# Two down projections of an MLP: seven block products in place of eight, on two of eight row groups of the weights

## The chip, the cores and the metric

One core of a Trainium2 chip runs the whole program. The metric is the device time of one execution in microseconds; the number given for a kernel is the median of several runs.

## The reference, cut to what matters

The program is one block with three attention branches, followed by two small transformer layers on 256 tokens of width 1024. Each of the two layers ends with the same MLP, and the change is in its second product:

```python
def sq_relu_mlp(x, w_up, w_down):
    h = jax.nn.relu(x @ w_up)
    return (h * h) @ w_down
```

x is 256 x 1024, w_up 1024 x 4096, w_down 4096 x 1024, all in float32. The result goes through a norm with a gain and is added to x.

## The kernel before

**Float32 by three products.** Every weight and every operand is cut into a rounded high part and a low part, the rest. A product is then high x high, high x low and low x high, three matmuls that add up in one PSUM bank. For a weight, ScalarE writes the high part `Wh` (`split`, L1294 to L1303) and VectorE subtracts it from the raw copy to get the low part `Wl` (`split`, L1828 to L1833).

**Granules and the ring.** The weights come from memory as one stream of granules of 1 MB: four blocks of 128 rows by 512 columns. `raw`, `Wh` and `Wl` have four slots each (`RING` = 4), granule g lies in slot g % 4. SP loads a slot of `raw` when VectorE has split the granule that was in it (`lo_ready`, L500 to L508). ScalarE may write a slot of `Wh` when TensorE has used up the granule four before (`gran_used`). TensorE waits for `lo_ready` of its granule.

**Units.** A unit is 512 output columns for both tiles of 128 tokens, so it owns a pair of PSUM banks `ps` (`bank(name, t)`); units alternate between the two pairs. A granule is 4 blocks x 3 matmuls x 2 token tiles = 24 matmuls of 128x512. `product` (L712) runs a unit granule by granule; `tile_by_tile` (L721) runs the last four granules of a stage first for token tile 0 and then for tile 1, so that the next stage can start on tile 0.

**The MLP.** The up product has eight units of two granules, `up{m}_0` to `up{m}_7` (m is 0 or 1). ScalarE reads each bank into `held` with a relu (L1721) and squares it (L1728). VectorE turns the squared rows in 32x32 blocks into `htmp` (`turn_pair`, L2382, 16 instructions for two units), ScalarE writes the high part `hTh` (`high_pair`, L1730) and VectorE the low part `hTl` (`low_pair`, L2396). The down product has two units of eight granules, `down{m}_0` and `down{m}_1`, 16 in all. Granule q of a unit needs the turned rows of group q (`h_low`). The last rows (groups 6 and 7) are turned and split while `down{m}_0` is already running. When unit 0 is done, ScalarE sums its squares (`down_squares`) and VectorE reads it out with the gain (`gained`); unit 1 ends with `normed_rows` and, in the first MLP, with `cross` into the next stage.

**The order of the work** is written out by hand for each engine and is strictly in order: ScalarE's in `mlp` (L1712), VectorE's in `mlp` (L2379), TensorE's in `mlp` (L1207). In `down{m}_0` both run a loop over the granules and split granule g + 4 while TensorE is at g. GpSimd has almost nothing to do in the MLP: the power -0.5 of the norms and the load of the next gain row (`after_mix`, L633). Four more PSUM banks, `aux0` to `aux3`, are used for transposes and attention, in an order fixed by `plan_aux` (L137); in the MLP they lie idle after the transposes of `x3T` or `x5T`.

## Time and profile before

| | us |
|---|---|
| median of 3 runs | 1108.35 (1107.96 to 1108.49) |
| profiled execution: span from the first to the last instruction | 1106.3 |
| TensorE busy in it | 1098.5 (99%) |
| TensorE weight loads | 913.3 (83%) |
| VectorE busy | 806.6 (73%) |
| ScalarE busy | 636.1 (58%) |
| GpSimd busy | 150.0 (14%) |
| memory read | 203.33 MB, 185 GB/s over the span |

Of the profiled execution only its span is given; the runs' times are from the device and lie 2.05 us above it. Times in the trace are counted from the start of the span. Matmuls overlap, so the mean duration of one (389 ns) is longer than the distance from one to the next; the path is read from the chain. The granted TensorE clock is 1.00 of full speed, 2.4 GHz, throughout. The first MLP's down units run from about 730 to 818, the second's from about 1013 to 1101. The profile marks VectorE as DVE, ScalarE as ACT, GpSimd as POOL, TensorE as PE and its weight load as PEld, and the queue of a sequencer by a q behind it.

### The profile page before, as it was taken

How to read it: one execution, taken by the hardware profiler on the slowest of the kernel's cores; microseconds unless marked ns; L12 is line 12 of the kernel's file. 1: busy time of each engine (PE TensorE's matmuls, PEld its weight loads, DVE VectorE, ACT ScalarE, POOL GpSimd, SP SyncE). 2: the span in 40 equal slices, each digit the busy share in tenths (PEclk: the TensorE clock that was granted, in tenths of full speed). 3: DMA queues.
4: the chain of work that ended last, by engine and by line, in shares of the span. 5: the costliest groups of instructions: out<-in, count | busy, mean ns of one | idle time of the engine just before them, and what ended most of it. 6: DMA issues, size and time to landing. Idle time of an engine off the chain costs nothing.

```text
span 1106.3 us, 13497 instructions
## 1 busy us (share of the span) xinstructions
PE 1098.5 (99%) x5131; PEld 913.3 (83%) x5131; DVE 806.6 (73%) x920; ACT 636.1 (58%) x787; POOL 150.0 (14%) x111
## 2 busy tenths in 40 slices
PE   9999999999999999999999999999999999999997
PEld 7788888888888888888888888888888888888886
DVE  5785768776678873778448569998467976899942
ACT  7656576655767653654587366654355655756431
POOL 1434600000344310000023000000005000000000
PEclk9999999999999999999999999999999999999999
DMA  9645444555455555655435446546555334654530
GB/s 355 247 172 183 144 161 162 200 190 190 186 195 190 190 195 185 229 200 197 183 115 195 166 179 258 188 156 229 193 188 208 122 145 171 225 174 180 191 145 38
DMA packets 30503, 205.16 MB, mean 185 GB/s; under 512 B 3624, under 2 KB 3792, under 8 KB 6768
## 3 DMA queue, kind: packets, MB, share of 16 engines
q1 hardware_dynamic: 28752, 198.75, 49.4%
q0 software_dynamic: 1696, 5.64, 1.6%
q8 instruction: 38, 0.62, 0.2%
q14 instruction: 17, 0.14, 0.0%
HBM read 203.33 MB, written 1.05 MB: 185 GB/s over the span
## 4 chain that ended last, share of the span: by engine, by line
PE 96%; DVE 2%; ACT 1%; issue 0%; DVEq 0%; ACTq 0%
PE ps L685 84%; PE ps L1139 3%; PE aux L757 3%; PE ps L1141 1%; PE ps L800 1%; PE aux L1006 1%; PE aux L1176 1%; PE aux L991 1%; PE ps L877 0%; PE aux L1163 0%; PE ps L793 0%; DVE Wl L1833 0%; ACT Wh L1303 0%; DVE prob L2050 0%; ACT bprob L1777 0%
## 5 line engine op out<-in xcount | busy, mean ns | idle before, releaser
L685 PE MATMUL ps<-Wh,xT 128*128 128x512 f32 x1792 | 560.1, 391 | 0.0
L1833 DVE TENSOR_TENSOR Wl<-raw,Wh 128x2048 fp32r<-128x2048 f32 x183 | 422.6, 2317 | 151.3 <-ACT Wh L1303 150.3
L1303 ACT ACTIVATE Wh<-raw 128x2048 fp32r<-128x2048 f32 x183 | 349.0, 1914 | 187.6 <-PE ps L685 187.5
L685 PEld LDWEIGHTS ps<-Wh,xT 128*128 128x128 f32 x1792 | 336.4, 188 | 69.9 <-issue 0.3
L685 PE MATMUL ps<-Wl,xT 128*128 128x512 f32 x896 | 348.6, 389 | 0.0
L685 PEld LDWEIGHTS ps<-Wl,xT 128*128 128x128 f32 x896 | 168.3, 188 | 34.1
L685 PE MATMUL ps<-Wh,hTh 128*128 128x512 f32 x256 | 99.7, 389 | 0.0
L685 PE MATMUL ps<-Wh,hTl 128*128 128x512 f32 x256 | 99.6, 389 | 0.0
L685 PE MATMUL ps<-Wl,hTh 128*128 128x512 f32 x256 | 99.6, 389 | 0.0
L2392 DVE STREAM_TRANSPOSE htmp<-held 32x512 f32<-32x512 f32 x128 | 90.0, 703 | 2.7
L637 POOL TENSOR_TENSOR sc<-sc,cst 128x1 f32<-128x1 f32 x8 | 4.5, 559 | 443.6 <-DVE sc L2352 443.6
L685 PEld LDWEIGHTS ps<-Wl,hTh 128*128 128x128 f32 x256 | 48.1, 188 | 10.0
L685 PEld LDWEIGHTS ps<-Wh,hTl 128*128 128x128 f32 x256 | 48.0, 188 | 10.0
L685 PEld LDWEIGHTS ps<-Wh,hTh 128*128 128x128 f32 x256 | 48.0, 188 | 9.8
L1139 PE MATMUL ps<-xT,Wh 128*128 128x512 f32 x128 | 45.3, 399 | 0.0
L521 POOL TENSOR_TENSOR sc<-sc,cst 128x8 f32<-128x8 f32 (+1 forms) x11 | 18.0, 1640 | 165.8 <-DVE sc L1900 153.9
L1721 ACT ACTIVATE held<-ps 128x512 f32<-128x512 f32 x32 | 18.8, 594 | 32.8 <-PE ps L685 32.8
L1141 PE MATMUL ps<-xT,Wl 128*128 128x256 f32 x128 | 35.9, 281 | 0.0
L685 PE MATMUL ps<-Wh,ffTh 128*128 128x512 f32 x88 | 34.4, 391 | 0.0
L685 PE MATMUL ps<-Wh,ffTl 128*128 128x512 f32 x88 | 34.3, 389 | 0.0
L685 PE MATMUL ps<-Wl,ffTh 128*128 128x512 f32 x88 | 34.2, 389 | 0.0
L1347 ACT ACTIVATE xT<-aux,gains 128x128 fp32r<-128x128 f32 x80 | 21.8, 384 | 21.6 <-PE aux L757 21.6
(355 smaller groups left out, 1310.6 us busy)
## 6 DMA issues: line engine op xcount, KB each, us to landing
raw<-in_wstream SPq DMA_DIRECT2D x185, 1024.0 KB, 4.8
grow<-in_post_gains POOLq DMA_DIRECT2D x4, 512.0 KB, 6.2
grow<-in_b_gate POOLq DMA_DIRECT2D x6, 256.0 KB, 3.4
mrows<-in_mem SPq DMA_DIRECT2D x2, 512.0 KB, 5.3
raw<-in_wstream SPq DMA_DIRECT2D x2, 512.0 KB, 6.5
x<-in_x SPq DMA_DIRECT2D x1, 1024.0 KB, 13.5
out<-x SPq DMA_DIRECT2D x4, 256.0 KB, 2.0
rdm<-in_ret_decays POOLq DMA_DIRECT2D x1, 768.0 KB, 5.1
```

The lines of the kernel that those rows point to most:

```text
L521: nc.gpsimd.tensor_tensor(S(f"{key}_rstd", 0, n), S(f"{key}_var", 0, n), K("minus_half").broadcast_to([P, n]), ALU.pow).then_inc(sem("norm ...
L685: mm = nc.tensor.matmul(ps[2 * pair + t][:, :], a[:, kt, t * P:(t + 1) * P], w[:, slot, j, :], start=(first and j == 0 and q == 0), stop=( ...
L757: tr = nc.tensor.transpose(o[0:src.shape[1], at:at + P], src, ident)
L800: mm = nc.tensor.matmul(bank("mk", t), a[:, 4 * g + j, t * P:(t + 1) * P], w[:, g, j, :], start=(g == 0 and j == 0 and a is memTh and w is ...
L991: mm = nc.tensor.matmul(o[:, t * TOK + k0:t * TOK + k1], qT[:, h + h0, t * P:(t + 1) * P], kT[:, h + h0, k0:k1], start=True, stop=True)
L1139: nc.tensor.matmul(o[:, :], Wh[:, g % RING, kt % 4, w], xT[:, kt, :, :], start=(kt == 0), stop=False, skip_group_check=True)
L1141: mm = nc.tensor.matmul(o[:, 0:TOK], Wl[:, g % RING, kt % 4, w], xTh[:, kt, :], start=False, stop=(kt == DK - 1), skip_group_check=True)
L1303: nc.scalar.activation(split_view(Wh, g), weight_view(raw, g), ACT.Copy).then_inc(hi_ready, 1)
L1347: nc.scalar.activation(dst[:, k0 + j, t * P:(t + 1) * P], o[:, j * P:(j + 1) * P], ACT.Copy, scale=gcol(gain, k0 + j)).then_inc(sem(f"{nam ...
L1721: nc.scalar.activation(held[:, n // 2, t, n % 2, :], bank(name, t), ACT.Relu).then_inc(drained["act"], 1)
L1833: nc.vector.tensor_tensor(split_view(Wl, g), weight_view(raw, g), split_view(Wh, g).bitcast(F32), ALU.subtract).then_inc(lo_ready, 1)
L2392: i = nc.vector.transpose(dst[b:b + 32, :, :, a:a + 32], src[a:a + 32, :, :, b:b + 32])
```

## The change

In each of the two down products, groups 0 and 1 of the rows of the weights, for both units, are a product of 2x2 blocks: A (two token tiles by two groups) times B (two groups by two units). Before, it is eight block products of 12 matmuls. After, it is seven, Q1 to Q7, by a form of Strassen's scheme, in which the weights are only added:

- the rows: Q1 takes a11, Q2 a12, Q4 a22; Q5 a21-a22, Q6 a11-a21+a22, Q7 a11-a21, Q3 a12-a11+a21-a22. The four mixed ones are made on VectorE (`mix_rows`, four subtractions on 128x512 in the up stage) and cut into high (`mixh`, ScalarE) and low parts (`mixl`, VectorE);
- the weights: Q1 B11, Q5 B11+B12, Q6 B11+B12+B22, Q4 the sum of all four; Q3 B22, Q7 B22+B12; Q2 B21. Q1, Q3 and Q2 are plain loads. Q5, Q6, Q4 and Q7 are transfers that GpSimd issues with an adding write onto the raw slot of the product four positions before (`fast_sums`);
- Q1, Q5, Q6 and Q7 go into the four `aux` banks, ScalarE copies each out (`fast_part`); Q2, Q3 and Q4 are added directly in the units' banks. GpSimd makes four sums of the copies, and VectorE adds them into the four banks (`add_part`): three before the split of the position behind Q7 plus four, one when unit 0 is complete;
- the order of TensorE is (0,2), (0,3), Q1, (1,2), (1,3), (0,4), Q5, (0,5), Q3, Q2, Q6, (0,6), Q7, (0,7), Q4, then granules 4 to 7 of unit 1 tile by tile; (n,q) is granule q of unit n. These are 19 positions of the ring in place of 16. TensorE waits for the added sums of unit 1 before its last four granules;
- SP's loop over the stream becomes a straight list, a plan of positions (`plan_positions`) takes the place of the granule numbers, the head norms share two semaphores, and the loops of VectorE and ScalarE over `down{m}_0` follow the new order.

The diff, cut to its core:

```diff
+FAST_ORDER = [(0, 2), (0, 3), "Q1", (1, 2), (1, 3), (0, 4), "Q5", (0, 5), "Q3", "Q2", "Q6", (0, 6), "Q7", (0, 7), "Q4"]
+FAST_LOAD = {"Q1": (0, 0, False), "Q5": (1, 0, True), "Q6": (1, 1, True), "Q4": (0, 1, True),
+             "Q3": (1, 1, False), "Q7": (1, 0, True), "Q2": (0, 1, False)}
+FAST_BANK = {"Q1": 0, "Q5": 1, "Q6": 2, "Q7": 3}
...
@@ SP
-            with sp.Fori(1, NG // RING) as i:
-                for j in range(RING):
-                    sp.wait_ge(lo_ready, i * RING + (j + 1 - RING))
-                    sp.dma_start(raw[:, j, :, :], by_ring[i, j]).then_inc(landed[j], 16)
...
+            for g in range(RING, NP):
+                if not ADDED[g]:
+                    sp.wait_ge(lo_ready, g + 1 - RING)
+                    sp.dma_start(raw[:, g % RING, :, :], wstream[SRC[g]]).then_inc(landed[g % RING], 16)
@@ GpSimd
+            def fast_sums(m):
+
+                first = P0[f"down{m}_0"]
+                for what in ("Q5", "Q6", "Q7", "Q4"):
+                    g = first + AT[what]
+                    pool.wait_ge(lo_ready, g + 1 - RING)
+                    pool.dma_start(raw[:, g % RING, :, :], wstream[SRC[g]], accum_op=ALU.add).then_inc(added[CHAIN[g]], 16)
+                wait_read(pool, f"fast{m}", FAST_BANK["Q1"])
+                wait_read(pool, f"fast{m}", FAST_BANK["Q6"])
+                nc.gpsimd.tensor_tensor(part6[:, :, :], part6[:, :, :], part1, ALU.subtract).then_inc(sem("fast_sum"), 1)
+                wait_read(pool, f"fast{m}", FAST_BANK["Q5"])
+                pool.wait_ge(sem("fast_sum"), 4 * m + 1)
+                nc.gpsimd.tensor_tensor(partu[:, :, :], part6[:, :, :], part5, ALU.add).then_inc(sem("fast_sum"), 1)
+                wait_read(pool, f"fast{m}", FAST_BANK["Q7"])
+                nc.gpsimd.tensor_tensor(part7[:, :, :], part7[:, :, :], part6[:, :, :], ALU.subtract).then_inc(sem("fast_sum"), 1)
+                pool.wait_ge(sem("fast_sum"), 4 * m + 3)
+                nc.gpsimd.tensor_tensor(part5, part5, part7[:, :, :], ALU.subtract).then_inc(sem("fast_sum"), 1)
@@ TensorE, mlp
-                product(f"down{m}_0", (hTh, hTl), before={q: rows_ready_for(q) for q in range(8)})
-                product(f"down{m}_1", (hTh, hTl), leave=RING)
...
+                fast_product(m, rows_ready_for)
+                before = {(0, 0): lambda: pe.wait_ge(sem("fast_add"), 4 * m + 2)}
@@ TensorE, fast_product, one product Q
+                        for j in range(4):
+                            if what in mixed:
+                                high, low = mixh[:, mixed[what], j, :], mixl[:, mixed[what], j, :]
...
+                            for i, (a, w) in enumerate(((high, Wh), (high, Wl), (low, Wh))):
+                                mm = nc.tensor.matmul(o, a, w[:, g % RING, j, :],
...
@@ ScalarE, mlp
                 for n in range(8):
                     up(n)
+                    if n == 7:
+                        split(P0[n0] + RING)
                     if n >= 3 and n % 2:
                         high_pair((n - 3) // 2)
                     squared_rows(n)
...
+                act.wait_ge(sem("mix_rows"), m + 1)
+                act.wait_ge(gran_used, P0[n0])
+                nc.scalar.activation(mixh[:, :, :, :], mixr[:, :, :, :], ACT.Copy).then_inc(sem("mix_high"), 1)
+                for k in range(1, len(FAST_ORDER)):
+                    if FAST_ORDER[k] in FAST_BANK:
+                        fast_part(FAST_ORDER[k], parts[FAST_ORDER[k]])
+                    elif k == 7:
                         high_pair(3)
...
+                    split(P0[n0] + k + RING)
@@ VectorE, mlp
+                def mix_rows():
+
+                    a11, a12 = htmp[:, 0:4, 0:P], htmp[:, 4:8, 0:P]
+                    a21, a22 = htmp[:, 0:4, P:TOK], htmp[:, 4:8, P:TOK]
+                    link(nc.vector.tensor_tensor(mixr[:, 0, :, :], a21, a22, ALU.subtract))
+                    link(nc.vector.tensor_tensor(mixr[:, 1, :, :], a11, mixr[:, 0, :, :], ALU.subtract))
+                    nc.vector.tensor_tensor(mixr[:, 2, :, :], a11, a21, ALU.subtract)
+                    nc.vector.tensor_tensor(mixr[:, 3, :, :], a12, mixr[:, 1, :, :], ALU.subtract).then_inc(sem("mix_rows"), 1)
...
+                for k in range(1, len(FAST_ORDER)):
+                    if k == AT["Q7"] + 1:
+                        dve.wait_ge(sem("fast_sum"), 4 * m + 4)
+                        add_part(n1, 0, partu[:, :, :])
+                        add_part(n1, 1, part5)
+                        wait_unit(dve, n0, 0)
+                        add_part(n0, 0, part1)
+                    split(P0[n0] + k + RING)
+                    if k in (1, 3, 4):
+                        at0 = {1: 4, 3: 8, 4: 12}[k]
+                        turn_pair(3, at0, at0 + 4)
+                    elif k == 2:
+                        dve.wait_ge(sem("mix_high"), m + 1)
+                        nc.vector.tensor_tensor(mixl[:, :, :, :], mixr[:, :, :, :], mixh[:, :, :, :].bitcast(F32), ALU.subtract)\
+                            .then_inc(sem("mix_low"), 1)
+                    elif k == 6:
                         low_pair(3)
...
+                wait_unit(dve, n0, 1)
+                add_part(n0, 1, part7[:, :, :])
+                gained(p, n0, 0, post_k)()
```

## Rows read from the trace of the kernel before

**Rows 1.** The page's part 4, the chain that ended last, by engine.
```profile
PE 96%; DVE 2%; ACT 1%; issue 0%; DVEq 0%; ACTq 0%
```

**Rows 2.** That chain in order of time, 700 to 925 us: start, duration, what.
```profile
699.96 112.20 PE ps L685 x495
```

**Rows 3.** Waits of PE over the span: total us, times, longest us.
```profile
PE ps L793 <- DVE warm L1934: 1.5, 1, 1.5
PE ps L685 <- DVE byTl L1852: 0.4, 1, 0.4
```

**Rows 4.** Windows: us, busy us (instructions) of PE, PEld, DVE, ACT, POOL, clock, DMA share, GB/s.
```profile
730.00:774.00 44.00, 44.00 (x196) 36.44 (x195) 40.24 (x35) 21.35 (x16) 0.00 (x0) 1.00 0.57 209
774.00:818.00 44.00, 44.00 (x200) 36.53 (x199) 20.25 (x20) 18.31 (x20) 0.56 (x1) 1.00 0.47 167
...
692.00:767.00 75.00, 75.00 (x333) 62.10 (x332) 73.70 (x70) 40.87 (x33) 0.00 (x0) 1.00 0.51 183
```

**Rows 5.** Groups by shape, 730 to 774 us: busy us, mean ns of one, idle before.
```profile
L1833 DVE TENSOR_TENSOR Wl<-raw,Wh 128x2048 fp32r<-128x2048 f32 x9 | 20.5, 2291 | 3.0 <-ACT Wh L1303 2.8
L1303 ACT ACTIVATE Wh<-raw 128x2048 fp32r<-128x2048 f32 x8 | 15.3, 1913 | 12.2 <-PE ps L685 12.2
L2392 DVE STREAM_TRANSPOSE htmp<-held 32x512 f32<-32x512 f32 x21 | 14.8, 703 | 0.4
...
L2401 DVE TENSOR_TENSOR hTl<-htmp,hTh 128x1024 fp32r<-128x1024 f32 x4 | 4.7, 1219 | 0.0
```

**Rows 6.** Groups by shape over the span: a 128x512 bank copy, a 128x512 VectorE product.
```profile
L1721 ACT ACTIVATE held<-ps 128x512 f32<-128x512 f32 x32 | 18.8, 594 | 32.8 <-PE ps L685 32.8
...
L2250 DVE TENSOR_TENSOR rcos<-reo,rtab 128x512 f32<-128x512 f32 x8 | 5.5, 692 | 0.3
```

**Rows 7.** Timeline of DVE in both MLPs: start, us, line, out, in, idle before.
```profile
730.53 2.29 DVE L1833 TENSOR_TENSOR Wl<-raw,Wh 128x2048 fp32r<-128x2048 f32 x1
...
763.35 4.49 DVE L1833 TENSOR_TENSOR Wl<-raw,Wh 128x2048 fp32r<-128x2048 f32 x2
770.68 2.29 DVE L1833 TENSOR_TENSOR Wl<-raw,Wh 128x2048 fp32r<-128x2048 f32 x1 [2.85 <-ACT Wh L1303]
...
1013.57 2.29 DVE L1833 TENSOR_TENSOR Wl<-raw,Wh 128x2048 fp32r<-128x2048 f32 x1
```

**Rows 8.** Timeline of ACT around the start of the first down unit.
```profile
730.60 0.60 ACT L1721 ACTIVATE held<-ps 128x512 f32<-128x512 f32 x1 [2.12 <-PE ps L685]
...
741.53 1.92 ACT L1303 ACTIVATE Wh<-raw 128x2048 fp32r<-128x2048 f32 x1 [1.02 <-PE ps L685]
746.98 1.92 ACT L1303 ACTIVATE Wh<-raw 128x2048 fp32r<-128x2048 f32 x1 [3.52 <-PE ps L685]
```

**Rows 9.** Timeline of DVE in the up stage: the first low_pair and what follows.
```profile
691.72 2.35 DVE L2401 TENSOR_TENSOR hTl<-htmp,hTh 128x1024 fp32r<-128x1024 f32 x2
694.18 2.85 DVE L2392 STREAM_TRANSPOSE htmp<-held 32x512 f32<-32x512 f32 x4
```

**Rows 10.** Timelines of POOL and DVE in the feed-forward stage: 128x512 products beside splits.
```profile
293.54 1.30 POOL L611 TENSOR_TENSOR gu<-gu 128x512 f32<-128x512 f32 x1 [2.83 <-DVE fe L1912]
294.97 3.19 POOL L615 TENSOR_TENSOR fheld<-gu,fe 128x512 f32<-128x512 f32 x1
...
294.34 5.96 DVE L1833 TENSOR_TENSOR Wl<-raw,Wh 128x2048 fp32r<-128x2048 f32 x2 [0.88 <-ACT Wh L1303]
...
336.39 3.28 POOL L611 TENSOR_TENSOR gu<-gu 128x512 f32<-128x512 f32 x1 [7.70 <-DVE fe L1912]
```

**Rows 11.** Transfers to landing: L505 (1 MB, SP); L642, L631 (512 KB, POOL); down window.
```profile
DMA to landing us min/median/max: 4.6/4.8/12.6
...
L642 POOL DMA_DIRECT2D grow<-in_post_gains x3: 572/572/617, 646.2 to 929.9; - x3
DMA to landing us min/median/max: 6.1/6.3/9.8
...
DMA to landing us min/median/max: 4.0/4.0/4.0
...
q1 hardware_dynamic: 1263, 9.17, 56.4%
```

More of the change, by code:

```diff
@@ L431, in build @@
         landed = [sem(f"landed{i}") for i in range(RING)]
+        added = [sem(f"added{i}") for i in range(2)]
         hi_ready = sem("hi_ready")
@@ L677, in _, with half_granule @@
         def _(pe):
-            def half_granule(slot, th, tl, kts, pair, t, first, last, ready=None):
+            def half_granule(slot, th, tl, kts, pair, t, first, last, ready=None, mixed=False):
                 for j, kt in enumerate(kts):
@@ L2206, in ff @@
                 name = f"ffn{n}"
[L2207 removed]
+                split(P0[name] + RING)
                 if first:
@@ L2426, in mlp, with add_part @@
                         turn_pair(k, 8, 12)
-                for g in range(G[f"down{m}_0"], GEND[f"down{m}_0"] - 1):
-                    split(g + RING)
-                    q = g - G[f"down{m}_0"]
-                    if q < 3:
-                        turn_pair(3, 4 * q + 4, 4 * q + 8)
-                    elif q == 3:
+                n0, n1 = f"down{m}_0", f"down{m}_1"
+                def add_part(name, t, part):
+                    v = bank(name, t).rearrange("p (k t) -> p k t", t=P)
+                    nc.vector.tensor_tensor(v, v, part, ALU.add).then_inc(sem("fast_add"), 1)
+                for k in range(1, len(FAST_ORDER)):
[14 more added lines that the diff above has]
+                    elif k == 6:
                         low_pair(3)
-                gained(p, f"down{m}_0", 0, post_k)()
-                split(GEND[f"down{m}_0"] - 1 + RING)
-                for g in range(G[f"down{m}_1"], GEND[f"down{m}_1"] - RING):
-                    split(g + RING)
+                wait_unit(dve, n0, 1)
+                add_part(n0, 1, part7[:, :, :])
+                gained(p, n0, 0, post_k)()
                 rows = normed_rows(p, f"down{m}_1", post_k, after)
                 if gain:
-                    cross(GEND[f"down{m}_1"], f"{after}T", gain, rows)
+                    cross(P1[f"down{m}_1"], f"{after}T", gain, rows)
                 else:
```

296 lines of the change are left out of this document (195 added, 101 removed).

## The prediction

> **What bounds the kernel now.** Three views in this order. The chain that ended last lies almost wholly on TensorE [rows 1]. Followed through the first MLP it is one unbroken run of matmuls, 495 in 112.20 us [rows 2], so a matmul costs 0.2267 us of the path (the 389 ns of the groups overlap), a granule of 24 costs 5.44 us and half a granule 2.72 us. TensorE hardly waits for a semaphore anywhere [rows 3]. A matmul that is left out in a down stage is therefore time gained, as long as its weights and operands come as early as before. The third view asks who would be late next. In the windows of the down stage VectorE is busy 40.24 of 44 us and ScalarE 21.35; from the middle of the up stage into the down stage VectorE is busy 73.70 of 75 us; in the second down unit it is busy 20.25 of 44 [rows 4]. So there are two limits close together: TensorE sets the end, and VectorE, in the very stretch that is changed, has almost nothing left.
>
> **What goes.** Per MLP, four granules (units 0 and 1, groups 0 and 1) of 24 matmuls become seven products of 12: 96 become 84. 12 x 0.2267 = 2.72 us per MLP, 5.44 us in both. With all of it: 1108.35 - 5.44 = 1102.9. (Sums are made on the span, 1106.3 us, which lies 2.05 us under the median of the runs; the difference is carried over unchanged.) The granted clock is 1.00 in all the windows [rows 4], so no gain or loss of clock enters.
>
> **What comes.** Time is counted from the start of the first down unit, 730.6, where ScalarE reads the last up bank [rows 8], and TensorE leaves a granule every 5.44 us (741.53, 746.98 there).
> TensorE, never waiting, would start the 15 positions at 0, 5.4, Q1 10.9, 13.6, 19.1, 24.5, Q5 29.9, 32.7, Q3 38.1, Q2 40.8, Q6 43.6, (0,6) 46.3, Q7 51.7, (0,7) 54.5, Q4 59.9, and the last four granules of unit 1 at 62.6. Each position needs its split (ScalarE 1.91, VectorE 2.29 us [rows 5]), and ScalarE may begin it only when TensorE has left the position four before.
>
> VectorE's queue. In the up stage four subtractions on 128x512 are put in (mix_rows), 4 x 0.69 [rows 6] = 2.8 us, and low_pair(0) loses half of one 1.22 us step, 0.5: +2.3 us in a queue without a gap [rows 4, 9]. The split of position 2 thus starts at 2.0 to 2.3 in place of -0.1 [rows 7]. From there to the split of position 11 the queue holds 10 splits x 2.29 (22.9), five groups of four transposes x 2.86 (14.3, from 703 ns each [rows 5]), two low_pairs x 2.35 (4.7) and the low part of the mixed rows, as large as a split (2.3): 44.2 us, done at 46.2 to 46.5. TensorE wants it at 46.3. All earlier positions have 1.6 us or more. So this place costs 0 to 0.2 us; each further microsecond of VectorE work ahead of it would cost nearly one. Before, the same queue ran out and waited for ScalarE only at 767.8 [rows 7].
>
> The accumulating transfers. Four of the seven weight sums are made by transfers of 1 MB that add onto a used raw slot. GpSimd issues each (0.57 us to issue [rows 11]) when VectorE has split the position four before. No row shows an accumulating transfer. The nearest below is a plain one of 1 MB, 4.8 us to landing (up to 12.6); the nearest above, twice the slowest 512 KB transfer of GpSimd, 2 x 9.8 = 19.6 us [rows 11]. In the down stage 9.17 MB took 56.4% of 44 us, 2.8 us of engine time per transfer of 1.05 MB; reading the old slot as well would add that once: 4.8 + 2.8 = 7.6; two full plain passes would be 9.6. I take 8 to 9, nearer the plain row because the size and pattern are the same. The Trainium skill, "Collectives: The Full Stack", Part 3, says of a reducing transfer that the add is free and "the add needs two source reads"; by that the estimate is 7.6 us and the whole gain, 1102.9; no run here shows it yet.
>
> What landing time L is allowed? Q5 has over 20 us, Q6 and Q7 about 12. The tight one is Q4. It is asked for when position 10 is split, at 41.5, issued by 42.5, and lands at 42.5 + L. ScalarE stands in its queue at this split; behind it stand the split of 15, the copy of Q7's bank (0.6 [rows 6]) and the split of 16: 3 x 1.9 + 0.6 = 6.3. Then VectorE splits 16 (2.3) and only then adds the shared sums into unit 1's two banks (2 x 0.69), for which TensorE waits before position 15. 42.5 + L + 6.3 + 2.3 + 1.4 = 52.5 + L against 62.6: a stall from L = 10.1 on, if GpSimd is quick.
>
> GpSimd's four sums of 128x512 take 1.30 us when VectorE stands or transposes, but 3.19 and 3.28 us beside a split, and two splits beside them took 5.96 in place of 4.49 us [rows 7, 10]. The last two sums (1.3 to 3.3 each) must lie between the copy of Q7, 55.1 at the earliest, and the adds: 57.7 to 61.7, plus 1.4, is 59.1 to 63.1 against 62.6. And each hit lengthens VectorE's queue by up to 1.3 us just where it works through 13 to 16; two of them move the point where the stall starts from L = 10.1 to about 7.5. So at L = 8 the stall is 0 to 0.6 us per MLP, at 9.6 it is 0 to 2.2. I take 0.6 each, 1.2 in all: 1102.9 + 1.2 = 1104.1.
>
> Edits that I cost at nothing, with their cover: the split of position 4 now stands ahead of high_pair(2) on ScalarE and holds it until 7.4, but its rows are wanted at 24.5 instead of 21.8; low_pair(3) ends at about 44 for a position at 46.3 (before it ended 763.3 for one at 763.3). The high part of the mixed rows (1.9 us) lies in ScalarE's idle time. SP's loop becomes a straight list and skips four transfers; its plain loads keep over 4.8 us except position 13 (asked 39.3, wanted 45.0), which may take about 8 us before it costs. On GpSimd the four issues and sums stand ahead of the power step of this MLP, which is wanted only after unit 1. The banks of the four own products are free since the transposes of x3. Unit 1's last granules, and all after them, run as before. The merged semaphores of the head norms change no order. The second MLP has the same queues at the same distances (VectorE's split of position 2 at 1013.57 [rows 7]), so each term counts twice.
>
> **The rivals.**
> 1. Nearly the whole gain: stall under 1.6 us per MLP, 1102.9 to 1106.1, likeliest 1104.1. For it: the counts above; against it: three places with less than 0.6 us of room.
> 2. The saved matmuls are handed back at the adds: L near 10 to 12 or GpSimd's last two sums caught beside splits. Stall 1.6 to 3.8 us per MLP, middle 2.6: 1102.9 + 5.2 = 1108.1, no change. For it: VectorE's full queue and the 3.28 us of a sum [rows 4, 10].
> 3. Slower, because an accumulating transfer is slow. From L = 12 on the splits of 11, 13 and 14 come late too and each late slot delays the one that waits for it, on top of the adds: walking the queues gives about 6 to 8.6 us per MLP at L = 14, 11 to 14 at 16. It decides from L of about 12.2, where the stall passes 2.7 + 1.1 us. At 14: 1102.9 + 2 x 7.3 = 1117.5. For it: GpSimd's own 512 KB transfers took 6.1 to 9.8 us in this kind of stretch and 4.0 in another [rows 11], and the adding itself could be slower than copying. The Trainium skill, "DMA: Bandwidth & Descriptors", section "SWDGE vs HWDGE vs iDMA", has a mechanism: descriptors issued by GpSimd are written into SBUF state from which VectorE can lock it out; with one split of wait, 2.3 us, the estimate would be L = 10.3 to 11, which is case 2; the spread of the rows fits it without proving it.
> 4. The matmuls go and the stretch does not shrink (a product into a fresh bank has a slower pitch). Nothing in the even pitch of [rows 2] speaks for it: in case 2's chance.
>
> **How the numbers follow.** Case 1: 0.54. Case 2 with 4: 0.21. Case 3: 0.25. A measurement of this kernel can tell about 0.2%, 2.2 us: faster is below 1106.1, slower above 1110.6. That makes faster 0.55, same 0.21, slower 0.24 (a little of case 3 ends inside). The prediction is case 1's, 1104.1. The range begins at 1102.5 (all of the gain, and 0.4 for the spread of the runs) and reaches into case 3 up to L of about 13.5, 1113; what is left out is about 0.16 above and 0.03 below.
>
> **What would show it.** TensorE has 24 matmuls fewer at the same pitch. Right: the accumulating transfers land in 7 to 10 us, TensorE's only new wait is one on the adds before position 15, under 1 us, and VectorE has no gap from 694 to about 780. Wrong in the way of case 2: that wait is 2 to 4 us and GpSimd's last sums take 3 us. Wrong in the way of case 3: ScalarE's splits of positions 10, 12 and 14 wait for a transfer, and TensorE waits for low parts at several positions. If a stall stands at position 11 alone, the cause is VectorE's load and mix_rows is what I sized too small.

## The result, and the profile after

The changed kernel took 1110.02 us (median of 13 runs, 1107.81 to 1114.02). The kernel before took 1108.20 us on the same chip (13 runs, 1107.96 to 1108.49). The ratio is 1.0019, 95% interval 1.0010 to 1.0028. The whole gain of the saved matmuls is gone, and the runs now differ from each other by 6 us where they differed by 0.5.

| | before | after |
|---|---|---|
| median, us | 1108.20 | 1110.02 |
| profiled execution, us (its span) | not given (1106.3) | 1108.16 (1106.3) |
| mean granted clock of the runs | 1.000 to 0.998 (64 runs beside the experiments) | 1.000 to 0.994 |
| matmuls | 5131 | 5107 |
| TensorE's waits for the adds, profiled run | none | 2.74 and 1.67 us |

The three runs of after whose mean granted clock is 1.000 took 1107.81, 1107.93 and 1108.16 us; all the others have 0.994 to 0.998 and took 1109.07 to 1114.02. So there are two things to explain: why the time at full clock is 1108 and not 1103, and what the clock does in the other runs. The profiled execution is one of the three, so its trace answers the first question only.

The mean clock has to be read with care. It is taken over the whole execution, and in every trace, also in that of the kernel before, the granted clock falls in the last microseconds, when TensorE has no matmul left. A run of the kernel before with 0.998 took 1108.00 us. So 0.998 alone doesn't show a drop inside the work; 0.997 and less, which four of the 13 runs have, stands in no run of the kernel before.

The waits of PE over the span, and the two waits in the first MLP as PE's timeline has them (start, us, line, operation). Against [rows 3] the first line is new:

```profile
PE ps L769 <- DVE ps L2600: 4.4, 2, 2.7
PE ps L878 <- DVE warm L2086: 1.5, 1, 1.5
PE ps L769 <- DVE byTl L2004: 0.4, 1, 0.4
```

```profile
793.00 0.39 PE L1318 MATMUL ps<-Wh,hTl 128*128 128x512 f32 x1
796.13 0.50 PE L769 MATMUL ps<-Wh,hTh 128*128 128x512 f32 x1 [2.74 <-DVE ps L2600]
```

L2600 is the add of a shared sum into a bank of unit 1. Up to 793.0 TensorE keeps its pitch, and the last matmul of Q4's twelve starts where the prediction's count puts it (730.6 + 62.6 = 793.2 for the next one). That next one starts at 796.13: 2.9 us are lost, and 0.1 on the following start. In the second MLP the last matmul starts at 1076.57 and the next at 1078.63, 1.9 us lost with the same 0.1 in it. Together 4.9, and 1102.9 + 4.9 = 1107.8. Position 11 adds under 0.2 us in each MLP (below), so this execution should take 1108.1, and it took 1108.16. The other two at 1.000 took 1107.81 and 1107.93.

The chain that ended last, in order of time, 780 to 797 us (start, us, what):

```profile
779.79 2.72 PE ps L769 x12
782.51 2.73 PE aux L1318 x12
...
785.70 1.90 ACT Wh L1435
787.60 0.48 ACT part L1879
788.09 0.07 issue
788.16 3.32 POOL part L724
791.48 0.07 issue
791.55 3.21 POOL spare L726
794.75 0.02 issue
794.78 1.31 DVE ps L2600 x2
```

Q7's product ends at 785.24. Its bank is copied only from 787.5, because ScalarE is in a split (1.90 us); then come GpSimd's two last sums, 3.32 and 3.21 us, and the two adds. VectorE's splits aren't in it: VectorE is done with them at 793.6 and waits 1.15 us for GpSimd. So the late transfer and the slow sums stand behind each other in one chain.

The windows that answer to [rows 4], in the same columns:

```profile
730.00:774.00 44.00, 44.00 (x196) 36.43 (x195) 43.41 (x38) 25.97 (x19) 3.50 (x4) 1.00 0.76 205
774.00:818.00 44.00, 41.26 (x185) 33.70 (x184) 30.68 (x29) 22.22 (x26) 11.21 (x5) 1.00 0.73 245
```

VectorE went from 40.24 to 43.41 of 44 us in the first, and TensorE is busy in all of it; in the second PE lacks 2.74. The transfer engines' share rose from 0.57 and 0.47 to 0.76 and 0.73, and in the 12 us in which Q4's transfer is under way it is 0.97 (the last number but one). That isn't special to Q4: the second line is a window in Q5's transfer, with 1.00. The third is the same window in the experiment without the adding, where more bytes moved in less time of the engines:

```profile
772.00:784.00 12.00, 12.00 (x54) 9.70 (x53) 9.15 (x6) 4.44 (x4) 4.42 (x3) 1.00 0.97 274
737.00:743.00 6.00, 6.00 (x28) 4.95 (x28) 5.95 (x5) 6.00 (x6) 0.00 (x0) 1.00 1.00 194
...
737.00:743.00 6.00, 6.00 (x28) 4.97 (x27) 5.96 (x5) 6.00 (x6) 0.00 (x0) 1.00 0.68 238
```

So a megabyte cost the transfer engines some 5.2 us with the adding (6.0 us at 1.00 and 194 GB/s) and 2.9 without it.

The adding transfers (L716). The page's row of all eight (KB each, median us to landing):

```profile
raw<-in_wstream POOLq DMA_DIRECT2D x8, 1024.0 KB, 8.1
```

The landing times of single ones, from the views of the tile: Q7's, Q4's in the first MLP, Q4's in the second.

```profile
DMA to landing us min/median/max: 8.1/8.1/8.1
DMA to landing us min/median/max: 11.4/11.4/11.4
DMA to landing us min/median/max: 10.3/10.3/10.3
```

ScalarE's timeline at the splits of positions 13 to 15:

```profile
777.75 1.92 ACT L1435 ACTIVATE Wh<-raw 128x2048 fp32r<-128x2048 f32 x1 [2.67 <-DMA raw<-in_wstream]
779.57 0.58 ACT L1879 ACTIVATE part<-aux 128x512 f32<-128x512 f32 x1
783.88 3.73 ACT L1435 ACTIVATE Wh<-raw 128x2048 fp32r<-128x2048 f32 x2 [3.73 <-DMA raw<-in_wstream]
787.51 0.57 ACT L1879 ACTIVATE part<-aux 128x512 f32<-128x512 f32 x1
```

Q4's transfer lands 11.4 us after its issue. ScalarE waits 3.73 us for it with two more splits and the copy of Q7 behind. GpSimd's timeline, and VectorE's, at the same time:

```profile
780.30 2.84 POOL L719 TENSOR_TENSOR part<-part,spare 128x512 f32<-128x512 f32 x1 [6.96 <-ACT part L1879]
783.28 1.30 POOL L722 TENSOR_TENSOR partu<-part,spare 128x512 f32<-128x512 f32 x1
788.16 3.31 POOL L724 TENSOR_TENSOR part<-part,part 128x512 f32<-128x512 f32 x1 [3.57 <-ACT part L1879]
791.55 3.20 POOL L726 TENSOR_TENSOR spare<-spare,part 128x512 f32<-128x512 f32 x1
```

```profile
779.70 2.29 DVE L1985 TENSOR_TENSOR Wl<-raw,Wh 128x2048 fp32r<-128x2048 f32 x1 [0.84 <-ACT Wh L1435]
785.83 7.80 DVE L1985 TENSOR_TENSOR Wl<-raw,Wh 128x2048 fp32r<-128x2048 f32 x3 [3.83 <-ACT Wh L1435]
```

The second sum lies in VectorE's gap and takes 1.30 us. The last two lie beside three splits and take 3.31 and 3.20, and those splits 7.80.

### The profile page after: what moved, and what is told of

Its sections match the earlier page's. It is cut to its first block, busy times and chain, and to the rows that moved or that the text cites. A ratio compares the mean times of both kernels' runs of the same rounds, so it can differ in the third digit from the quotient of the medians.

```text
span 1106.3 us, 12943 instructions
## 1 busy us (share of the span) xinstructions
PE 1094.1 (99%) x5107; PEld 908.6 (82%) x5107; DVE 834.6 (75%) x944; ACT 653.3 (59%) x803; POOL 178.4 (16%) x127
## 4 chain that ended last, share of the span: by engine, by line
PE 86%; DVE 9%; ACT 2%; POOL 1%; issue 1%; DMA 1%; DVEq 0%; ACTq 0%
PE ps L769 72%; DVE Wl L1985 3%; DVE htmp L2546 3%; PE ps L1224 3%; PE aux L842 3%; PE ps L1226 1%; ACT Wh L1435 1%; PE ps L885 1%; PE aux L1318 1%; DMA raw<-in_wstream 1%; PE aux L1091 1%; PE aux L1261 1%; POOL part L724 1%; POOL spare L726 1%; PE aux L1076 1%
## 5 line engine op out<-in xcount | busy, mean ns | idle before, releaser
L1985 DVE TENSOR_TENSOR Wl<-raw,Wh 128x2048 fp32r<-128x2048 f32 x189 | 437.4, 2326 | 128.0 <-ACT Wh L1435 127.0
L1435 ACT ACTIVATE Wh<-raw 128x2048 fp32r<-128x2048 f32 x189 | 360.3, 1914 | 184.3 <-PE ps L769 165.7
L769 PE MATMUL ps<-Wh,hTh 128*128 128x512 f32 x192 | 75.2, 392 | 4.4 <-DVE ps L2600 4.4
L769 PE MATMUL ps<-Wh,hTl 128*128 128x512 f32 x192 | 74.7, 389 | 0.0
L769 PE MATMUL ps<-Wl,hTh 128*128 128x512 f32 x192 | 74.7, 389 | 0.0
L769 PEld LDWEIGHTS ps<-Wh,hTh 128*128 128x128 f32 x192 | 36.0, 188 | 13.2 <-DVE ps L2600 5.3
L716 POOL DMA_DIRECT2D raw<-in_wstream x8 | 7.0, 875 | 245.3 <-DVE Wl L1985 245.3
L769 PEld LDWEIGHTS ps<-Wh,hTl 128*128 128x128 f32 x192 | 36.0, 188 | 7.5
L769 PEld LDWEIGHTS ps<-Wl,hTh 128*128 128x128 f32 x192 | 36.1, 188 | 7.4
L691 POOL TENSOR_TENSOR RG<-RG,rge 128x1024 f32<-128x1024 f32 x4 | 13.7, 3424 | 129.1 <-ACT rge L1424 129.1
```

Of the source, the lines that this page charges most:

```text
L691: nc.gpsimd.tensor_tensor(RG[:, h, :, :], RG[:, h, :, :], rge[:, :, :], ALU.mult).then_inc(sem("rg_silu"), 1)
L769: mm = nc.tensor.matmul(ps[2 * pair + t][:, :], a[:, kt, t * P:(t + 1) * P], w[:, slot, j, :], start=(first and j == 0 and q == 0), stop=( ...
L1435: nc.scalar.activation(split_view(Wh, g), weight_view(raw, g), ACT.Copy).then_inc(hi_ready, 1)
L1985: nc.vector.tensor_tensor(split_view(Wl, g), weight_view(raw, g), split_view(Wh, g).bitcast(F32), ALU.subtract).then_inc(lo_ready, 1)
```

## The experiments

The theory that the result suggests: the gain goes back at the adds (case 2), by two causes that meet, Q4's late transfer and GpSimd's two late sums; and the idle stretch of TensorE then often brings a drop to the lower clock. Times are medians. Where runs are compared, each is measured against the kernel before on its own chip, whose median was 1108.12 to 1108.15 us in all of them.

### The changed kernel again, for another trace

> The changed kernel again, unaltered, for its clock and a second trace. Two things are to be told apart in its runs. Theory P (waits only): with the granted clock at 1.000 it takes 1107.9, the same as before, because TensorE's waits at the adds (3 and 2 us in the two MLPs) hand back the 5.4 us of the left-out matmuls. Theory C (clock): what lies above 1107.9 in a run is a stretch at the lower clock and nothing else; then each run's time follows its mean clock, about 1.1 us for 0.001, and runs with clock 1.000 all lie at 1107.8 to 1108.2. Rival to C: transfers that land late in some runs; then times spread at clock 1.000 too.

It took 1110.58 us (12 runs, 1106.38 to 1116.14), ratio 1.0021 (1.0007 to 1.0035). Theory C holds in the large: the four runs at a mean clock of 0.996 took 1111.10 to 1112.49 us and the one at 0.994 1116.14, and no run at 0.999 or 1.000 took over 1108.21. Its rival has a part too: those four at 0.999 and 1.000 differ by 1.8 us (1106.38 to 1108.21), more than the clock can explain, so the waits themselves vary from run to run. This profiled execution, 1109.57 us, shows what the first did not. TensorE's wait in the first MLP is 2.27 us. PE's timeline behind it, and the windows (columns as in [rows 4]):

```profile
795.73 0.50 PE L769 MATMUL ps<-Wh,hTh 128*128 128x512 f32 x1 [2.27 <-DVE ps L2600]
...
796.53 0.47 PE L769 MATMUL ps<-Wh,hTh 128*128 128x512 f32 x1
796.80 0.63 PE L769 MATMUL ps<-Wl,hTh 128*128 128x512 f32 x1
```

```profile
795.00:796.00 1.00, 0.27 (x1) 0.27 (x2) 1.00 (x3) 0.47 (x1) 0.00 (x0) 1.00 0.90 377
796.00:797.00 1.00, 1.00 (x5) 0.79 (x5) 1.00 (x2) 0.69 (x2) 0.00 (x0) 0.85 1.01 410
797.00:798.00 1.00, 1.00 (x3) 0.79 (x3) 1.00 (x1) 0.08 (x1) 0.00 (x0) 0.50 0.32 123
798.00:799.00 1.00, 1.00 (x4) 0.73 (x3) 1.00 (x2) 0.00 (x0) 0.00 (x0) 0.50 0.02 8
```

The granted clock falls to 0.50, which is 1.2 GHz in place of 2.4, about 1 us after TensorE has begun again, though it is busy without a gap by then. A matmul now takes 0.63 us in place of 0.39, and the pitch is 0.427 in place of 0.227. Eight matmuls later it is back at 1.00. That costs 8 x 0.2 = 1.6 us. The two waits of this execution cost 2.5 and 2.15 us and position 11 0.35 in all, and 1102.9 + 4.65 + 0.35 + 1.6 = 1109.5, against its 1109.57. The second MLP's wait (1.9 us) was followed by no drop.

### The four transfers write in place of adding

```
-                    pool.dma_start(raw[:, g % RING, :, :], wstream[SRC[g]], accum_op=ALU.add).then_inc(added[CHAIN[g]], 16)
+                    pool.dma_start(raw[:, g % RING, :, :], wstream[SRC[g]]).then_inc(added[CHAIN[g]], 16)
```

> The four transfers of GpSimd per MLP write in place of adding, so the weight sums are left out; everything else is as in the changed kernel. Theory P1 (the adding transfer is the cause: it reads twice and keeps the transfer engines at 0.99 busy): landing falls from 8.1 to 11.4 us to 5 to 6, ScalarE no longer waits for a transfer, the copy of Q7 moves from 2.3 us after the product to 0.1, and the wait at the adds falls from about 3 and 2 us to under 1 each: 1103.5 to 1105 where the clock holds. Rival P2 (GpSimd's sums alone are the cause): landing falls but the wait stays above 2 us, 1107 to 1108.

What this kernel leaves out is the weight sums. 1104.11 us (4 runs, 1104.08 to 1104.24), ratio 0.9964 (0.9949 to 0.9978). The same queue, the same places and the same neighbours, and the landing of all eight is

```profile
DMA to landing us min/median/max: 4.9/4.9/5.0
```

Nobody waits for them, and the runs lie within 0.2 us. GpSimd's last sums still take 2.88 and 3.22 us, but from 786.02 on, 2.1 us earlier. TensorE's first matmul behind the adds starts 0.3 us late in each MLP (793.60 and 1074.53), too little to be listed as a wait. So the adding costs 3 us of landing at Q5 to Q7 and 5 to 6 us at Q4, and without it the slow sums fit but for 0.3 us.

### GpSimd's last two sums left out

```
-                wait_read(pool, f"fast{m}", FAST_BANK["Q7"])
-                nc.gpsimd.tensor_tensor(part7[:, :, :], part7[:, :, :], part6[:, :, :], ALU.subtract).then_inc(sem("fast_sum"), 1)
-                pool.wait_ge(sem("fast_sum"), 4 * m + 3)
-                nc.gpsimd.tensor_tensor(part5, part5, part7[:, :, :], ALU.subtract).then_inc(sem("fast_sum"), 1)
...
-                        dve.wait_ge(sem("fast_sum"), 4 * m + 4)
+                        dve.wait_ge(sem("fast_sum"), 2 * m + 2)
+                        wait_read(dve, f"fast{m}", FAST_BANK["Q7"])
```

VectorE now waits for the copy of Q7 itself; two of the four corrections are missing from the result.

> GpSimd's third and fourth sums are left out (two of the four corrections are then missing from the result); VectorE adds as soon as Q7's bank is copied. Theory P2 (GpSimd's sums of 3.3 and 3.2 us are the last link): the wait at the adds falls to about 1 us in the first MLP and less in the second, limited by VectorE's splits of positions 14 to 16: 1103.5 to 1105.5 where the clock holds. Rival P1 (the landing of Q4 alone decides): the wait stays at 2 us or more, 1106.5 to 1108.

1103.53 us (5 runs, 1103.34 to 1105.37), ratio 0.9963 (0.9950 to 0.9975). The transfers are as slow as ever (7.8 to 10.6 us, and ScalarE waits 3.44 us for Q4's), but the adds come at 791.8, and PE has no wait for them. VectorE's timeline at the splits that took 7.80 us in the kernel after:

```profile
785.16 6.70 DVE L1981 TENSOR_TENSOR Wl<-raw,Wh 128x2048 fp32r<-128x2048 f32 x3 [3.54 <-ACT Wh L1431]
791.78 0.69 DVE L2596 TENSOR_TENSOR ps<-ps,partu 128x512 f32<-128x512 f32 x1
```

Three splits take 6.70 without a GpSimd sum beside them: the two sums cost VectorE 1.1 us. Either cause alone, then, is nearly harmless; the stall needs both.

### All four sums on VectorE

GpSimd's four sums go. VectorE does the first two ahead of its split of position 14, and the last two directly ahead of the second add. The edit changes a second thing: both adds into unit 1 move from behind the split of position 16 to ahead of it.

```
+                    if k == AT["Q6"]:
+                        for q in ("Q1", "Q5", "Q6"):
+                            wait_read(dve, f"fast{m}", FAST_BANK[q])
+                        link(nc.vector.tensor_tensor(part6[:, :, :], part6[:, :, :], part1, ALU.subtract))
+                        link(nc.vector.tensor_tensor(partu[:, :, :], part6[:, :, :], part5, ALU.add))
+                    if k == AT["Q7"]:
+                        add_part(n1, 0, partu[:, :, :])
+                        wait_read(dve, f"fast{m}", FAST_BANK["Q7"])
+                        link(nc.vector.tensor_tensor(part7[:, :, :], part7[:, :, :], part6[:, :, :], ALU.subtract))
+                        link(nc.vector.tensor_tensor(part5, part5, part7[:, :, :], ALU.subtract))
+                        add_part(n1, 1, part5)
                     if k == AT["Q7"] + 1:
-                        dve.wait_ge(sem("fast_sum"), 4 * m + 4)
-                        add_part(n1, 0, partu[:, :, :])
-                        add_part(n1, 1, part5)
```

(In this loop an index k splits the position k + 4, so these stand ahead of the splits of positions 14 and 16.)

> The four sums move from GpSimd to VectorE: the first two before its split of position 14, where it waits for ScalarE anyway, the last two and the adds of unit 1 before the split of position 16. Nothing is left out. If the waits at the adds are the whole loss, they go to under 0.5 us and the kernel takes 1103 to 1104 with the clock at 1.000. Theory C1 (TensorE's waits of 2 to 3 us bring the lower clock): no run has a clock under 1.000 any more and the median is 1103 to 1104. Rival C2 (the lower clock has another cause in the changed stretch, such as all engines and transfers being busy at once): runs with clock 0.994 to 0.998 stay as frequent, and the median lies 1 to 3 us above the fastest.

1103.13 us (5 runs, 1103.06 to 1104.22), ratio 0.9955 (0.9942 to 0.9968). This computes everything and beats both kernels by 5 and 7 us. The sums, on VectorE's timeline:

```profile
791.13 0.69 DVE L2590 TENSOR_TENSOR ps<-ps,partu 128x512 f32<-128x512 f32 x1
791.73 0.68 DVE L2601 TENSOR_TENSOR part<-part,part 128x512 f32<-128x512 f32 x1
792.45 0.69 DVE L2602 TENSOR_TENSOR spare<-spare,part 128x512 f32<-128x512 f32 x1
793.17 0.70 DVE L2590 TENSOR_TENSOR ps<-ps,spare 128x512 f32<-128x512 f32 x1
```

0.69 us each, in place of 3.2 on GpSimd and what that takes from the splits. Q4's transfer lands after 12.1 us here, no sooner than before, and PE waits 0.41 us, in one MLP. 0.2 us are left of the stall.

How much of this is the engine and how much the new place of the adds wasn't measured apart. An estimate from the trace of the experiment before this one: its adds begin at 791.8, behind the split of position 16, and the second ends at 793.1. Two sums of 0.7 us ahead of them would make it 794.5, where TensorE wants them at 793.3. So on VectorE but behind that split, about 1 us of stall would be left per MLP at Q4's 10.6 us, and more at 12.1; the move ahead of the split (2.29 us) takes that away.

Theory C1 is met in the median and the spread. That no run lies under a mean clock of 1.000 is not: four of the five have 0.999, as most runs of the kernel before do.

### TensorE's wait filled with matmuls

```
+                def filled():
+                    g = P0[f"down{m}_1"]
+                    wait_low_part(g)
+                    wait_read(pe, f"fast{m}", FAST_BANK["Q1"])
+                    o = aux[AUX[(f"fast{m}", FAST_BANK["Q1"])][0]]
+                    for i in range(12):
+                        nc.tensor.matmul(o[:, :], hTh[:, 16 + i % 4, 0:P], Wh[:, g % RING, i % 4, :], start=True, stop=True)
+                    pe.wait_ge(sem("fast_add"), 4 * m + 2)
...
+                before = {(0, 0): filled}
```

> The changed kernel, and where TensorE would stand idle for the adds (2.3 to 2.7 us in the run that showed the lower clock) it now runs twelve more 128x512 products into a bank that nobody reads any more; nothing that the result needs changes. Theory A (the idle wait itself brings the drop to the lower clock behind it): the wait is filled, the mean clock stays at 0.999 or 1.000 in all runs, the times lie within 1 us of each other and the median is 1107.6 to 1108.8, which is the changed kernel's time at clock 1.000. Theory B (the drop comes from something else in this stretch, such as the heavy mix of engines at work): the runs keep their spread of several us, and the median stays near 1110. If twelve products (12 x 0.227 = 2.7 us) are more than the wait was, the second MLP's wait of about 2 us is overfilled by 0.5 to 1 us, which is in the upper end of A's figure.

1109.09 us (11 runs, 1108.39 to 1110.36), ratio 1.0009 (1.0000 to 1.0018). The mean clocks are 0.998 to 1.000 in all runs, where 9 of the 25 runs with the wait open have 0.994 to 0.997. The spread is 2.0 us in place of 6.2 and 9.8. That is theory A's answer. The clocks carry it and not the spread, since 2.72 us of filling also swallow waits that vary in length. The median lies 0.3 us above theory A's upper end: the filling costs a full 2 x 2.72 us whenever it is longer than the wait, 1102.9 + 5.4 = 1108.3. Of what lies above that, up to 2 us, a part is outside the span: the slowest two runs have spans of 1107.4 and 1108.5 us, and one of them lies 3.0 us above its span where most lie 1.9 above. The rest isn't explained by the trace of the one profiled run, in which no wait for the adds is left.

### The adds later, and no GpSimd: two, four and eight more VectorE subtractions

Made from the version with all sums on VectorE, ahead of the second add (2 stands for 2, 4 or 8):

```
+                        for _ in range(2):
+                            link(nc.vector.tensor_tensor(part6[:, :, :], part6[:, :, :], part1, ALU.subtract))
```

> The variant with all four sums on VectorE (1103.13), and in each MLP two more 128x512 subtractions on VectorE ahead of the second add, which repeat a sum whose result is not read: 2 x 0.69 = 1.4 us later for the adds. TensorE's wait there was 0.4 us, so it should be about 1.8 us in each MLP. The waits alone would make 1103.1 + 2.8 = 1105.9. Theory A (the idle wait brings the lower clock): few or no runs below clock 0.999, since the wait is under the 2.3 us that was followed by a drop; at most one run in three stands 1 to 3 us above the rest. Theory B (it is GpSimd's late sums or the late transfer, not the wait): no drop at all, 1105.9 in every run.

> As the one with two more subtractions, with four: 4 x 0.69 = 2.8 us later for the adds, a wait of about 3.2 us in each MLP, and no sum on GpSimd. The waits alone would make 1103.1 + 5.5 = 1108.6. Theory A (the idle wait brings the lower clock): most runs have a mean clock of 0.994 to 0.998, the windows behind the wait show 0.50 for some 4 us, and the times spread over 2 to 6 us above 1108.6. Theory B (the drop needs GpSimd's sums or the late transfer): clock 0.999 to 1.000 in all runs and 1108.6 within 0.5 us.

> As the one with four more subtractions on VectorE ahead of the second add, with eight. There TensorE waited 1.1 and 1.7 us; four more of 0.72 us make 4.0 and 4.6 us. No sum is on GpSimd. The waits alone would make 1102.9 + 8.6 = 1111.5. Theory A (the idle wait itself brings the lower clock): the windows behind the waits show a granted clock of 0.50 for some us, the mean clock of most runs lies at 0.997 or under, and the median stands 2 to 4 us above 1111.5. Theory B (the drop needs GpSimd's sums or the late adding transfer): 1.00 behind both waits and 1111.5 within 0.7 us.

| more subtractions | median, us (range, runs) | mean clocks | PE waits in the profiled run, us |
|---|---|---|---|
| 0 | 1103.13 (1103.06 to 1104.22, 5) | 0.999 to 1.000 | 0.41, none |
| 2 | 1104.24 (1103.92 to 1106.67, 7) | 0.998 to 1.000 | 0.64, none |
| 4 | 1107.94 (1105.13 to 1110.55, 11) | 0.996 to 1.000 | 1.1, 1.72 |
| 8 | 1117.16 (1112.85 to 1119.24, 6) | 0.993 to 0.998 | 4.77, 3.59 |

The waits of the first two were shorter than expected, and so were the times (1104.24 and 1107.94 against 1105.9 and 1108.6). The expectations started from the 0.41 us of wait in the version without extra work, but in that trace Q4's transfer had landed after 12.1 us, and in the first MLP of these two after 10.8 and 9.8: VectorE's split of position 14 began at 785.17 and 784.40 in place of 786.72. The spread grows with the wait, 1.2, 2.8, 5.4 and 6.4 us, and no GpSimd sum is left in any of them. The landing of Q4's transfer, which differs by up to 2.3 us from one of these traces to the next, can hold a part of it, and does with four: two runs at a mean clock of 1.000 took 1105.13 and 1107.05. The mean clocks go down with the wait too. With four the mean clock reaches 0.996 in the slowest run, but the profiled one shows no drop behind its waits of 1.1 and 1.7 us; its mean of 0.998 comes from the end, where TensorE has stopped. So with four neither theory is met as written. With eight the trace shows the drop behind both waits. PE's timeline and windows of the variant with eight:

```profile
792.91 0.39 PE L1308 MATMUL ps<-Wh,hTl 128*128 128x512 f32 x1
798.07 0.80 PE L759 MATMUL ps<-Wh,hTh 128*128 128x512 f32 x1 [4.77 <-DVE ps L2590]
```

```profile
793.00:797.00 4.00, 0.29 (x2) 0.00 (x0) 3.83 (x6) 1.91 (x1) 0.00 (x0) 1.00 0.49 205
797.00:798.00 1.00, 0.00 (x0) 0.00 (x0) 0.97 (x3) 0.00 (x0) 0.00 (x0) 0.72 0.00 0
798.00:804.00 6.00, 5.93 (x14) 4.68 (x15) 6.00 (x5) 0.78 (x2) 0.00 (x0) 0.50 0.46 143
...
1085.00:1091.00 6.00, 5.61 (x13) 4.46 (x14) 6.00 (x5) 0.78 (x2) 0.00 (x0) 0.50 0.00 0
```

Here the waits cost 4.9 and 3.8 us, and at 0.50 fifteen matmuls from 798.07 to 804.48 took 6.4 us in place of 3.4, thirteen in the second MLP 2.7 too much: 1102.9 + 8.7 + 3.0 + 2.7 = 1117.3, against the 1117.51 of this execution. The median is 5.7 us above 1111.5, more than theory A's 2 to 4. Theory B falls as far as GpSimd's sums go: the drop doesn't need them. The filled wait shows the other side: without the idle stretch no mean clock is under 0.998, though the sums and the late transfer are there.

The Trainium skill, "TensorE: Matmul & The Clock Gate", Part 1, knows these two levels, 1.2 and 2.4 GHz, and says that the lower is the default, which activity releases. The windows agree: 0.50 and 1.00 with mixtures of both at the edges only, and the fall behind an idle stretch. But the length of the wait alone doesn't decide: of the two traces of the changed kernel the one with 2.27 us shows a drop and the one with 2.74 us none, and what decides it no run here shows.

### Three more VectorE operations among the mixes

Made from the version with all sums on VectorE:

```
+                    for _ in range(3):
+                        link(nc.vector.tensor_tensor(mixr[:, 3, :, :], a12, mixr[:, 1, :, :], ALU.subtract))
```

> The variant with all four sums on VectorE (1103.13), and in each MLP three more 128x512 subtractions on VectorE among the mixes, ahead of the splits of positions 10 and 11; they repeat a mix that is written over with the same values. It measures the step of the prediction that says that VectorE's queue is level with TensorE at position 11 (46.2 to 46.5 against 46.3), so that each microsecond ahead of it costs nearly one. That step gives 3 x 0.69 = 2.1 us of stall less 0.2, so about 1.9 us in each MLP and 1103.1 + 3.8 = 1106.9, with TensorE waiting for VectorE's split of position 11. The rival, that VectorE has 2 us or more to spare there, gives 1103.1 to 1103.6 and no such wait.

1107.60 us (11 runs, 1107.48 to 1109.51), ratio 0.9994 (0.9985 to 1.0003): 4.5 us more than without them, where 3.8 were expected, 2.2 per MLP for 2.1 us of work. The profiled run is the slowest one, at a mean clock of 1.000; from the first 25 us on it runs 1.8 us behind the trace of the version without the three, long before the MLPs. Its waits of PE for VectorE's splits (total us, times, longest), positions 11 and 9:

```profile
PE ps L759 <- DVE Wl L1975: 2.1, 2, 1.0
PE ps L1308 <- DVE Wl L1975: 1.6, 2, 0.8
```

VectorE had no time to spare: every microsecond of work put ahead of position 11 comes out at the end. The first of the two waits in order of time is at position 9 (0.8 us), so that there some 1.3 us were free, not the 1.6 or more of the prediction; the second, at position 11, adds the rest. The clocks of all runs are 0.998 to 1.000, so waits of 0.8 and 1.0 us brought no drop that the times show.

### The loads behind Q4's transfer cut to a quarter

```
+                    k = 1 if any(g - P0[f"down{m}_0"] in (15, 16) for m in range(2)) else 4
-                    sp.dma_start(raw[:, g % RING, :, :], wstream[SRC[g]]).then_inc(landed[g % RING], 16)
+                    sp.dma_start(raw[:, g % RING, 0:k, :], wstream[SRC[g], :, 0:k, :]).then_inc(landed[g % RING], 16)
```

> The changed kernel, but the two plain loads that follow Q4's adding transfer (positions 15 and 16) move a quarter of their megabyte each, so their products are not the reference's. It tells why Q4's transfer lands after 10.3 to 11.4 us where the others take 8. Theory C (it shares the transfer engines with these loads): Q4's lands after 8 to 9 us, its splits start 2 to 3 us earlier, TensorE's wait for the adds goes from 2.3 to 2.7 down to under 0.8 us, and the time is 1103.2 to 1105. Theory D (an adding transfer is slow there by itself, or by the loads of positions 13 and before): it lands after 10 us or more, and the time stays at 1107.6 to 1110.

The weights of these two positions are in part missing. 1107.74 us (10 runs, 1104.53 to 1109.43), ratio 0.9997 (0.9988 to 1.0006). Q4's transfer landed after

```profile
DMA to landing us min/median/max: 9.8/9.8/9.8
```

in both MLPs, against 11.4 and 10.3; ScalarE's split of it began 1.8 us earlier (782.09), and PE's waits were 1.21 and 1.14 us in place of 2.74 and 1.67. Four of the ten runs have a mean clock of 0.997. Neither theory is met. With the loads whole, the nine traces of the kernels that add have Q4's between 8.7 and 12.1 us, 14 of 18 over 10, so the quarter loads took at most some 1 us off, and 2 us over the 7.9 of the other adding transfers remain. The plain load of position 13 is the nearest suspect. It is issued 2.5 us before Q4's, and in all these traces it is still under way in the first 3.2 to 5.6 us of it; the shortest of these overlaps goes with the 8.7 us and the longest with the 12.1, and most between are in order. With quarter loads the overlap is 4.5 us and Q4's takes 9.8, where whole loads at the same overlap give 10.2 to 10.6. That fits a sharing of the transfer engines, but both transfers would be slowed by a third cause as well, and no run left this load out: the cause stays open.

## Why the prediction was wrong

It forecast 1104.1, and the gain did not come. It had the right place, the right price of the matmuls and, as its second case, the right mechanism, and gave the first case the better chance. The step that failed is the size of the stall at the adds: 0.6 us per MLP were taken, 3.0 and 1.9 were measured, by two terms that are taken up below, and a drop of the clock came on top that had been put at nothing.

- **The saved matmuls: right.** 24 fewer, pitch 0.227 us. The version with all sums on VectorE, where little of the stall is left, has 1103.06 us as its fastest run against the 1102.9 of the sum.
- **VectorE's queue at position 11: right.** The timeline has the splits of 11 and 12 as one entry of 4.49 us from 774.37, so that of 11 ends at 776.7, 46.1 us from the start; the prediction said 46.2 to 46.5, and TensorE wanted it at 46.3. Its first two matmuls there come 0.1 us late each, under the 0 to 0.2 that the step allows, and the three added operations cost 2.2 us per MLP.
- **The landing time L: the step that failed, in one place of four.** L was one number, 8 to 9, for all four transfers. Q5's, Q6's and Q7's land after 8.0 to 8.4. Q4's, the only one that matters, lands after 11.4 and 10.3 us. The prediction worked out that Q4's was the tight one, and yet did not ask what else moves at 772 to 784, where one plain load is under way when it is issued and three more follow before it has landed. The bound from above (19.6) contained it; the value taken, "nearer the plain row because the size and pattern are the same", did not. Plain transfers in Q4's place landed in 5.0 us, so it is the adding that is sensitive; why Q4's more than the others is open (the quarter loads).
- **GpSimd's last two sums: sized too small by their place.** They were put at 57.7 to 61.7, between the cheap and the dear figure, each 1.3 to 3.3, from a copy of Q7 at 55.1, as if this path did not depend on L. But they follow on the copy of Q7, which stood behind ScalarE's late splits (done at 57.5 in the trace), and at that time VectorE has three splits in a row. They took 3.31 and 3.20 us and ended at 64.2 (794.75). The clash with the splits was in the text, which lets two of them move the point where the stall starts from L = 10.1 to about 7.5; by that very line L = 10.3 to 11.4 gives 2.8 to 3.9 us, and 1.9 and 3.0 were measured. That it comes so near is partly luck: the line makes VectorE's queue longer by up to 1.3 us for each sum, and the trace shows 0.55 each and a VectorE that waits 1.15 us for GpSimd. The 0.6 us that was taken for each stall is the term that was wrong: 1.2 us in all against 4.9.
- **The Trainium skill on the transfer.** By the Trainium skill, "Collectives: The Full Stack", Part 3, "the add needs two source reads", and the estimate from it was 7.6 us; Q5's to Q7's show 8.0 to 8.4, and the engine time of a megabyte, 5.2 us against 2.9, agrees with a second read. By the Trainium skill, "DMA: Bandwidth & Descriptors", section "SWDGE vs HWDGE vs iDMA", the estimate was 10.3 to 11 (one split on 8 to 9 is 10.3 to 11.3), which is near what Q4's shows, but not by its mechanism as far as the traces go: a plain transfer from the same queue in the same place lands after 5.0 us with the same VectorE splits around it. The section also ties the lock to a 2-port mode of VectorE, and no run here shows that the splits use it.
- **"No gain or loss of clock enters": wrong.** It held for the kernel before, whose TensorE hardly waits. The change made an idle stretch of 2 to 3 us; a drop to the lower clock behind it is shown in one of the two traces of this kernel and costs 1.6 us there, and mean clocks of 0.994 to 0.997 speak for it in 9 of 25 runs. The median of 1110.02 lies 2.2 us above 1107.8 and the slowest run 6; how much of the 2.2 is the clock and how much a longer wait, no trace shows. Together they carried the result from the middle of "no change" to its upper edge.
- **Case 3 did not come:** no add transfer made TensorE wait for a low part, and the walk of the other queues held. The plain load of position 13 landed late (ScalarE waited 2.67 us at 775.1 to 777.75), without cost.

## What to carry to other kernels

Where several queues meet in one place, take each duration from rows of that very stretch, with what runs beside it then, and not as one value for the kernel: the one transfer of four that had the least room was the slow one, and a GpSimd operation on 128x512 cost 1.30 us or 3.3 by its neighbour. Two causes of lateness that lie behind each other add up, and taking away either one was nearly enough. A short sum that a critical add waits for can be cheaper on VectorE, even where that engine is nearly full (0.69 us against 3.2), and the add belongs ahead of any split that isn't wanted sooner; the two together were worth 5 to 7 us of the whole. And a new wait of 2 to 5 us on a busy TensorE can cost about 1.6 times its length, because the granted clock may fall behind it (2.5 and 1.6 us more; 8.7 and 5.7 more). A mean clock that sinks below that of the kernel before is the sign of it; a growing spread alone can also be waits that vary.

## What the runs showed of the hardware

- A transfer of 1 MB that adds onto SBUF lands after 7.7 to 8.4 us where the same without adding lands after 4.9, and after 8.7 to 12.1 in Q4's place, beside up to four plain loads. It costs the transfer engines some 5.2 us in place of 2.9. To issue it keeps GpSimd for 0.87 us, in place of 0.53.
- GpSimd's 128x512 sum takes 1.30 us beside an idle VectorE and 2.8 to 3.3 beside its splits, which take 0.55 us longer for it. The Trainium skill, "SBUF — State Buffer", section "SBUF: two separate sides", describes an exclusive lock on a shared pair of ports, taken among others by VectorE operations with two SBUF inputs, for which the other engine waits; 1.30 plus most of a split of 2.29 us is about 3.3, which agrees for GpSimd. For VectorE the traces show less: a wait for a whole sum would be 1.3 us, and 0.55 are measured.
- The granted clock fell to 0.50 after an idle stretch of 2.3 us, about 1 us after work had begun again, and stayed there for 3.4 us (eight matmuls). After 4.8 and 3.6 us of waiting it fell while TensorE still stood, and came back 6.2 and 5.6 us after work had begun. After a wait of 2.7 us in another run it did not fall.
